# A transformer block in split fp32: one 512-column product for both parts of x in the gate and up tiles

## The reference

```python
def swiglu(x, w_gate, w_up, w_down):
    return (jax.nn.silu(x @ w_gate) * (x @ w_up)) @ w_down
```

## Time and profile before

| | |
|---|---|
| median of 3 runs | 3036.05 us (3034.6 to 3036.47) |
| profiled execution | span 3033.5 us, 64798 instructions |
| PE busy | 2858.9 us, 94% |
| DVE busy | 1641.2 us, 54% |
| ACT busy | 1220.4 us, 40% |
| chain that ended last | PE 81%, DVE 13%, ACT 3% |

### The profile page before, as it was taken

The page is one execution under the profiler, slowest core; times in us unless marked ns, Lnnn a source line. Parts: engine busy times, 40 slices in busy tenths (PEclk is TensorE's granted clock), DMA queues, the critical chain, the costliest instruction groups (busy, mean ns, idle before and its releaser), DMA issues.

```text
span 3033.5 us, 64798 instructions
## 1 busy us (share of the span) xinstructions
PE 2858.9 (94%) x27888; PEld 2392.3 (79%) x27888; DVE 1641.2 (54%) x2465; ACT 1220.4 (40%) x1864; POOL 112.1 (4%) x152
## 2 busy tenths in 40 slices
PE   8999999999999999998868999998998999998998
PEld 8987799899877997776656777785456998985986
DVE  5546655454565555213564777646234564565885
ACT  5445554444455545322443432334103434432333
POOL 0000000000000000000000000000001222220000
PEclk9999999999999999997988999999999999999999
DMA  6544345554543454441001333321210000003443
GB/s 251 181 176 163 137 153 182 180 181 176 185 153 124 175 182 150 181 153 70 2 10 56 120 144 141 123 87 62 84 56 16 5 5 24 5 4 112 140 153 111
DMA packets 50412, 349.82 MB, mean 115 GB/s; under 512 B 5840, under 2 KB 5840, under 8 KB 9808
## 3 DMA queue, kind: packets, MB, share of 16 engines
q1 hardware_dynamic: 49680, 343.56, 31.8%
q0 software_dynamic: 448, 2.11, 0.2%
HBM read 344.61 MB, written 1.05 MB: 114 GB/s over the span
## 4 chain that ended last, share of the span: by engine, by line
PE 81%; DVE 13%; ACT 3%; issue 2%; DMA 1%; DVEq 0%; ACTq 0%; SPq 0%
PE psum L165 80%; DVE arena L98 3%; DVE ring_low L87 2%; DVE arena L87 2%; DVE wide L87 2%; DMA ring<-in_evt 1%; PE psum L170 1%; DVE wide L98 1%; DVE ring L87 1%; ACT w_high L144 1%; ACT wide L138 0%; ACT arena L140 0%; ACT x_high L138 0%; ACT arena L144 0%; DVE arena L94 0%
## 5 line engine op out<-in xcount | busy, mean ns | idle before, releaser
L87 DVE TENSOR_TENSOR ring_low<-ring,w_high 128x2048 fp32r<-128x2048 f32 (+3 forms) x254 | 560.3, 2206 | 554.1 <-ACT w_high L144 549.3
L144 ACT ACTIVATE w_high<-ring 128x2048 fp32r<-128x2048 f32 (+3 forms) x254 | 468.9, 1846 | 766.0 <-PE psum L165 452.9
L165 PE MATMUL psum<-x_high,w_high 128*128 128x256 f32 (+1 forms) x2040 | 632.8, 310 | 8.1 <-DVE arena L87 6.3
L165 PE MATMUL psum<-x_high,ring_low 128*128 128x256 f32 (+1 forms) x2040 | 625.9, 307 | 0.0
L165 PE MATMUL psum<-x_low,w_high 128*128 128x256 f32 (+1 forms) x2040 | 625.7, 307 | 0.0
L165 PEld LDWEIGHTS psum<-x_high,w_high 128*128 128x128 f32 x2040 | 389.5, 191 | 45.6 <-issue 17.1
L165 PEld LDWEIGHTS psum<-x_high,ring_low 128*128 128x128 f32 x2040 | 389.6, 191 | 18.4
L165 PEld LDWEIGHTS psum<-x_low,w_high 128*128 128x128 f32 x2040 | 389.7, 191 | 16.8
L165 PE MATMUL psum<-wide,ring 64*64 64x64 f32 (+3 forms) x3888 | 384.4, 271 | 12.2 <-DVE wide L87 7.6
L165 PEld LDWEIGHTS psum<-wide,ring 64*64 64x64 f32 (+2 forms) x3888 | 269.6, 147 | 108.6 <-issue 78.0
L165 PE MATMUL psum<-w_high,x_high 128*128 128x512 f32 (+2 forms) x720 | 282.2, 392 | 10.4 <-issue 8.0
(11 more groups left out here) (196 smaller groups left out, 3421.1 us busy)
## 6 DMA issues: line engine op xcount, KB each, us to landing
ring<-in_f_gu SPq DMA_DIRECT2D x88, 1024.0 KB, 4.8
ring<-in_w_mod SPq DMA_DIRECT2D x48, 1024.0 KB, 5.0
ring<-in_fu SPq DMA_DIRECT2D x44, 1024.0 KB, 4.8
ring<-in_f_dn SPq DMA_DIRECT2D x40, 1024.0 KB, 4.8
ring<-in_w_in SPq DMA_DIRECT2D x28, 1024.0 KB, 4.8
ring<-in_fd SPq DMA_DIRECT2D x20, 1024.0 KB, 4.9
ring<-in_rkvr SPq DMA_DIRECT2D x12, 1024.0 KB, 4.8
ring<-in_w_out SPq DMA_DIRECT2D x8, 1024.0 KB, 4.9
```

Of the source, the lines that this page charges most:

```text
L87: self.done(self.eng.tensor_tensor(o, a, b, op), then)
L144: self.done(self.eng.activation(o, i, ACT.Copy, scale=scale), then)
L165: ins = self.eng.matmul(o, l, r, start=a, stop=z)
```

## The change

The two parts of x become two halves of one tensor `x_both`. For each k, the high weights multiply both parts in one product of 512 columns, which fills the bank: columns 0 to 255 collect the products with high x, columns 256 to 511 those with low x. The low weights multiply high x as before, into columns 0 to 255. The two halves of a bank are then added: ACT copies the second half out (`half_out`, into `ghalf` or `uhalf`), and DVE adds that copy to the first half (`halves_added`, into `gsum` or `usum`). Silu reads `gsum` and the product `usum`, both in SBUF. The four new buffers are double. The feed-forwards 4 and 5 keep the three products.

```diff
-        x_high = at("x_high", [128, 4096], XHIGH, F32R)
-        x_low = at("x_low", [128, 4096], XLOW, F32R)
+        x_both = at("x_both", [128, 2, 4096], XHIGH, F32R)
+        x_high, x_low = x_both[:, 0, :], x_both[:, 1, :]
...
-                    T.bank(b, prod_ok[i, f] if half else (silu_ok[i, f] if i < 4 else img_ok[i, f]))
+                    T.bank(b, (usum_ok if half else gsum_ok)[i, f] if i < 4 else prod_ok[i, f] if half else img_ok[i, f])
...
+                        wide_product(T, b, wt, o, k, k == 0, k == 7, then)
...
+        def wide_product(T, b, wt, o, k, first, last, then):
+
+            both = x_both[:, :, 256 * k:256 * k + 256]
+            if first:
+                T.mm(bank(b), wt[0][:, o:o + 128], both, True, False)
+            T.mm(bank(b)[:, 0:256], wt[1][:, o:o + 128], both[:, 0, :], False, False)
+            if not first:
+                T.mm(bank(b), wt[0][:, o:o + 128], both, False, last, then)
+
+        def half_out(A, o, b, then):
+            A.copy(o, bank(b)[:, 256:512], then)
+
+        def halves_added(D, o, b, half, then):
+            D.tt(o, half, bank(b)[:, 0:256], ALU.add, then)
...
-                se.wait_ge(*gate_mm[i, f])
                 if i < 4:
+                    se.wait_ge(*gate_mm[i, f])
+                    if f >= 2:
+                        se.wait_ge(*gsum_ok[i, f - 2])
+                    half_out(A, ghalf[:, f % 2, :], 2 * (f % 3), ghalf_ok((i, f)))
+                    if f:
+                        high_part(A, i, f - 1)
+                    se.wait_ge(*gsum_ok[i, f])
                     if f >= 4:
                         se.wait_ge(*prod_ok[i, f - 4])
-                    A.act(sil[:, f % 4, :], bg[:, 0:256], ACT.Silu, silu_ok((i, f)))
+                    A.act(sil[:, f % 4, :], gsum[:, f % 2, :], ACT.Silu, silu_ok((i, f)))
...
                 if i != 5 and (i, f) != (4, 21):
                     split_on(split_act, A, ("gu", i, f))
+                if i < 4:
+                    if f >= 2:
+                        se.wait_ge(*usum_ok[i, f - 2])
+                    se.wait_ge(*w_free["gu", i, f])
+                    half_out(A, uhalf[:, f % 2, :], 2 * (f % 3) + 1, uhalf_ok((i, f)))
...
                 if i < 4:
+                    ve.wait_ge(*ghalf_ok[i, f])
+                    if f >= 2:
+                        ve.wait_ge(*silu_ok[i, f - 2])
+                    halves_added(D, gsum[:, f % 2, :], 2 * (f % 3), ghalf[:, f % 2, :], gsum_ok((i, f)))
+                    ve.wait_ge(*uhalf_ok[i, f])
+                    halves_added(D, usum[:, f % 2, :], 2 * (f % 3) + 1, uhalf[:, f % 2, :], usum_ok((i, f)))
                     ve.wait_ge(*silu_ok[i, f])
-                    ve.wait_ge(*w_free["gu", i, f])
                     if f >= 4:
                         ve.wait_ge(*hh_ok[i, f - 4])
-                    D.tt(product_of(i, f), sil[:, f % 4, :], bank(2 * (f % 3) + 1)[:, 0:256], ALU.mult, prod_ok((i, f)))
+                    D.tt(product_of(i, f), sil[:, f % 4, :], usum[:, f % 2, :], ALU.mult, prod_ok((i, f)))
                     if f:
                         low_part(D, i, f - 1)
```

More of the change, by code:

```diff
@@ L614, in program @@
         prod_ok = signal("prod_ok", [(i, f) for i in FFNS for f in range(22)])
+        gsum_ok, usum_ok = [signal(n, [(i, f) for i in range(4) for f in range(22)]) for n in ("gsum_ok", "usum_ok")]
+        ghalf_ok, uhalf_ok = [signal(n, [(i, f) for i in range(4) for f in range(22)]) for n in ("ghalf_ok", "uhalf_ok")]
         hh_ok = signal("hh_ok", [(i, u) for i in FFNS for u in range(12 if i == 4 else 22)])
@@ L621, in program @@
         prod = arena[:, 12288:13312].rearrange("p (a t) -> p a t", a=4)
+        gsum = arena[:, 16384:16896].rearrange("p (a t) -> p a t", a=2)
+        usum = arena[:, 16896:17408].rearrange("p (a t) -> p a t", a=2)
+        ghalf = arena[:, 17408:17920].rearrange("p (a t) -> p a t", a=2)
+        uhalf = arena[:, 17920:18432].rearrange("p (a t) -> p a t", a=2)
         hT = arena[:, 0:11264].rearrange("p (k t) -> p k t", k=22)
@@ L677, in ffn_pe @@
                             continue
-                        mms(T, products(bank(b)[:, 0:tok], [y[:, o:o + 128] for y in wt],
-                                        [x_hi[:, k, :], x_lo[:, k, :]], k == 0, k == 7),
-                            None if k < 7 else w_free(key) if half else gate_mm((i, f)))
+                        then = None if k < 7 else w_free(key) if half else gate_mm((i, f))
+                        if i >= 4:
+                            mms(T, products(bank(b)[:, 0:tok], [y[:, o:o + 128] for y in wt],
+                                            [x_hi[:, k, :], x_lo[:, k, :]], k == 0, k == 7), then)
+                            continue
+                        wide_product(T, b, wt, o, k, k == 0, k == 7, then)
                 if i == 4:
@@ L760, in ffn_act @@
                     split_on(split_act, A, ("gu", i, f))
-                if f and i != 4:
+                if f and i == 5:
                     high_part(A, i, f - 1)
```

## The result

The changed kernel takes 3171.62 us (median of 4 runs, 3163.85 to 3173.12), the kernel before 3035.32 in the same session (4 runs, 3032.6 to 3036.47). The ratio is 1.0441, 95% interval 1.0428 to 1.0454: slower by 136 us, where 131.6 was forecast.

The account below looks back on a forecast made before the run. The prediction took PE to bound the kernel, and the change to make an ACT-DVE ring of waits the bound: span 3033.5 + 131.6 = 3165.1 us, plus 2.55 for the median, so 3168 us, range 3142 to 3190.

Parts of the forecast that it names:

- The bound before: Feed-forward gate and up tiles: PE sets the pace at 5.76 us a tile, ACT and DVE idle about half.
- PE's part: Per k, products of 512 and 256 columns replace three of 256: tile from 5.76 to 5.55 us, 18.5 over 88.
- The ring: ACT and DVE wait on each other in each gate and up tile: 6.68 us work plus 0.80 between, 7.48.
- The silu's signal: From DVE's gate sum to ACT's silu, which waits for three semaphores: 0.10 us taken.
- When it sets in: PE's stalls in a feed-forward begin with tile 5 or 6; the first tiles run on splits made ahead.
- The sum: Added time of 32.9 us for each feed-forward, 131.6 us for four, on the profiled span of 3033.5.
- the mean is 6.7: Time from a feed-forward's first product to its first gate sum: 6.7 us on the mean over four.
- Signs that came out otherwise: PE gaps about 1.9 us before tiles; gate and up stages some 27 us longer, first three down tiles 6.
- 6.75: Time in us from the first gate sum to the end of tile 3's low split.
- the bound stayed with PE: Rival: ACT and DVE keep ahead of PE, 3018 us or 3036; chance 0.05 of gain, 0.01 within 0.2%.
- The clock hardly fell: Rival: PE's idle time in feed-forwards lowers its clock to 0.71, costing 25 us more, 3193; chance 0.08.
- The ring was not shorter than its parts: Rival: steps between instructions vanish, a turn takes 6.68 us, 70 us less in all, 3098; chance 0.03.

Follow-up runs that it names:

- PE's part alone: Kernel before with only the wide product added, no halves copied or added, silu and product reading the first half: 3023.62 us, ratio 0.9954.
- the copy moved alone: Changed kernel with ACT's copy of the up half put ahead of the high split: 3028.4 us, ratio 0.9966 to the kernel before.
- the copy outside the ring: Changed kernel with ACT's copy of the gate half made twice, where ACT otherwise waits for DVE: 3165.69 us, ratio 1.043 to the kernel before.
- two products of 256: Changed kernel with each 512-column product issued as two of 256 columns: 3162.0 us, ratio 1.0418 to the kernel before.
- a copy more in the ring: Changed kernel with ACT's copy of the up half made twice: 3207.17 us, ratio 1.0567 to the kernel before.

## Why the prediction was right

- **The bound before**: as read. PE's part alone gained 14 us and showed that PE's tile was the pace.
- **PE's part**: the sign and the size were right, the term a little too large. Expected 5.55 us a tile from the steps of 0.120 and 0.227; measured 5.59 in the three kernels with the wide product in which PE is the bound. A product of 512 beside one of 256 takes 0.35 us for the pair, not 0.347. By an estimate from the Trainium skill's figure ("TensorE: Matmul & The Clock Gate", Part 1: some 2.5 ns a product beyond its columns) the merge would have saved 3.5 us in all. The runs do not agree: 14 us were measured, with an interval of 9 to 19 us, and 0.17 us a tile over 16 merges are 11 ns for each.
- **The ring**: forecast 7.48 us a tile, measured 7.47. The parts agree too: silu from SBUF 0.42, copy 0.39, sums 0.42, low split to gate sum 0.13 (98.11 + 2.29 to 100.53). The silu's signal took 0.03 (100.95 to 100.98), not the 0.10 taken for its three semaphores; the steps into the product (0.14 for 0.11) and the high split (0.12 for 0.10), and 0.01 each on three durations, gave that back.
- **When it sets in**: forecast tile 5 or 6, seen ahead of tile 5.
- **The sum**: forecast 131.6 us for four feed-forwards. Feed-forward 0 began at 18.40 us instead of 18.09, and its part can be read from the start of the loads for the mixer behind it in SP's timeline: 220.73 instead of 186.12, 34.6 later. By the prediction's own terms this one should be 34.0 longer, since its first sum comes 7.86 us after its first product where the mean is 6.7. The stretches of loads that hold feed-forwards 1, 2 and 3 are 31.4, 32.6 and 32.8 us longer (349.52 to 575.84 became 384.10 to 641.78, 575.84 to 770.43 became 641.78 to 868.98, 935.32 to 1160.52 became 1034.98 to 1292.98), 131.4 for all four. With the stages between and behind them, the load for the recurrent mixer's weights is issued at 2403.61 instead of 2270.61, 133.0 later. The rest of the 136 us arises behind that, where the code is unchanged (below).
- **Signs that came out otherwise**: the prediction expected gaps of about 1.9 us before PE's tiles, and gate and up stages 27 us longer with another 6 in the first three down tiles. The gaps recorded are 1.6 us (the ends of products are modelled in the profile; the starts on either side, 98.46 and 100.45, are 1.99 apart, where 0.24 is an ordinary step). In feed-forward 0 the first down product came 157.1 us after the first gate product instead of 127.0, so 30.1 us of the cost stand ahead of it and 4.2 behind. The prediction's own terms put it 28.7 later on the mean (6.7 + 6.75 + 19 x 7.48 + 0.14 = 155.7, less 127.0), so its 27 and 6 were misreckoned; the total is not touched by that. Some turns are longer too, 7.87 us for instance (low splits at 45.42 and 53.29). Why is open.
- **The rivals**: the bound stayed with PE only in the kernels in which the order was mended (with the copy moved alone PE's work and the ring of 5.86 are nearly even). The clock hardly fell: it is 1.00 in the gate and up stages of feed-forwards 0 and 1 and 0.99 in those of 2 and 3 (1130 to 1170 us has 0.96), well above the 0.74 below which the prediction had it cost time. The ring was not shorter than its parts.

Since all of this was expected, the experiments mostly confirm; what they add is the price of the order itself, and a version that keeps PE's gain.

## What to carry to other kernels

Added work that fits an engine by its occupancy can still set the pace: write down, for one period, which instruction waits for which and what stands ahead of it on its engine, and look whether the arrows close. If they do, the period is the sum around the ring, and double buffers do not shorten it when each wait is for the same tile. The remedy shown here is an order in which the short instruction whose result the other engine waits for goes ahead of the long one (here a split) that nobody waits for so soon: the copy ahead of ACT's split, or the gate sum ahead of DVE's. Taking a 2.29 us split out of the ring by moving one 0.42 us addition was worth 146 us.

## What was not expected of the hardware

An unchanged stage differs by several microseconds between executions. In SP's timeline the stretch from the second load ahead of the recurrent scan to the first load behind it is, in the kernel before,

```profile
2270.61 14.06 SPq L3259 DMA_DIRECT2D ring<-in_rw  x2
2523.89 0.33 SPq L3259 DMA_DIRECT2D ring<-in_rwo  x1
```

253.3 us long, and in the changed kernel

```profile
2403.61 14.06 SPq L3300 DMA_DIRECT2D ring<-in_rw  x2
2661.55 0.33 SPq L3300 DMA_DIRECT2D ring<-in_rwo  x1
```

257.9 us; in the kernel with the copy outside the ring it is 252.7. This is one part of why kernels with the same turn of 7.47 us lie between 3162 and 3172 us, and not the whole. The span of the kernel with the copy outside the ring is 10.0 us shorter than that of the changed one: 3.0 lie ahead of the second block, 2.6 between there and the scan, 5.2 in the scan, and behind it 0.8 are lost again. For the kernel with two products of 256, 11.1 us shorter, these parts are 3.9, 4.0 and 1.5 us, and 1.7 behind the scan. Why the stages vary is open.

In the kernel with a copy more in the ring, where PE idles longest, the mean granted clock from 24 to 140 us, in feed-forward 0, was 0.94, where all the other kernels have 1.00, so part of it ran at the 1.2 GHz level:

```profile
24.00:140.00 116.00, 97.60 (x506) 82.01 (x505) 57.71 (x72) 58.45 (x91) 0.00 (x0) 0.94 0.43 149
```

It cost nothing that can be seen: the feed-forwards took 36 us more than in the change (1328.68 less 1292.98), and 37 are explained by the turn. That fits what the prediction argued against its rival: a slower PE only uses up idle time that it has.
